# Finer waits ahead of seven TensorE products, and VectorE for the last imaginary part

## The reference

```
h = layer_norm(x)
for l in 0, 1:
    h = layer_norm(A*h + hybrid_mixer(h))            # three attention branches a, b, c, each projected, gated, summed
    h = layer_norm(A*h + memory_cross_attention(h))  # keys and values from 'mem' (256 x 1024)
    h = layer_norm(A*h + ffn)                        # l = 0: swiglu; l = 1: mixture of 8 experts
x = x + rmsnorm(even_mixer(rmsnorm(x)))              # dilated attention of 16 heads beside a state-space scan
x = x + rmsnorm(odd_mixer(rmsnorm(x)))               # pooling over windows, a gate, one last product
```

## Time and profile before

| | us |
|---|---|
| median of 3 runs | 2126.41 (2125.18 to 2128.82) |
| the profiled execution | 2124.61 |
| its span, first to last instruction | 2122.8 |

### The profile page before, as it was taken

One profiled execution on the slowest core, in us unless ns is written; L12 is line 12 of the kernel. 1 busy time (PEld: TensorE's weight loads), 2 busy tenths in 40 slices (PEclk: granted clock), 3 DMA queues, 4 the chain that ended last, 5 costly groups with the idle time before them and its releaser, 6 DMA issues.

```text
span 2122.8 us, 30291 instructions
## 1 busy us (share of the span) xinstructions
PE 2096.0 (99%) x13540; PEld 1251.1 (59%) x13540; DVE 785.6 (37%) x1430; ACT 323.9 (15%) x700; POOL 65.5 (3%) x72
## 2 busy tenths in 40 slices
PE   8999999999999999999999999999999999999998
PEld 4888786997468869753333333333333544855997
DVE  4325645556642276550100002001000489344446
ACT  2332121110123301210000000000000232420200
POOL 0000000000000000000000000000000035000000
PEclk9999999999999999999999999999999999999999
DMA  7524544444344245059999996999999832326340
GB/s 303 224 76 159 199 159 159 159 159 153 144 168 165 85 166 205 1 227 370 383 399 382 405 395 280 371 381 396 383 403 399 335 122 99 120 76 241 109 169 20
DMA packets 38453, 485.60 MB, mean 229 GB/s; under 512 B 4480, under 2 KB 4640, under 8 KB 7088
## 3 DMA queue, kind: packets, MB, share of 16 engines
q1 hardware_dynamic: 34848, 464.66, 54.8%
q0 software_dynamic: 3472, 18.95, 2.3%
HBM read 482.54 MB, written 1.05 MB: 228 GB/s over the span
## 4 chain that ended last, share of the span: by engine, by line
PE 92%; DVE 5%; ACT 1%; issue 1%; DMA 0%; POOL 0%; SPq 0%; DVEq 0%; ACTq 0%
PE bank L379 50%; PE pair L379 42%; DVE att L2411 2%; DVE att L2500 1%; DVE prob L2513 0%; DMA weights<-in_moe_down 0%; DVE prob L2411 0%; DVE att L2491 0%; DVE probT L2411 0%; DVE probT L2513 0%; ACT hT L2718 0%; DVE big L2461 0%; ACT big L2702 0%; DVE att L1584 0%; DMA const<-in_const 0%
## 5 line engine op out<-in xcount | busy, mean ns | idle before, releaser
L379 PE MATMUL bank<-weights,att 128*32 128x512 f32 (+1 forms) x4228 | 460.7, 593 | 0.3 <-DVE att L1584 0.2
L379 PEld LDWEIGHTS bank<-weights,att 128*32 128x32 f32 (+1 forms) x4228 | 137.6, 110 | 307.0 <-issue 307.0
L379 PE MATMUL bank<-hT,weights 128*128 128x256 f32 (+1 forms) x1232 | 246.9, 358 | 0.0
L379 PEld LDWEIGHTS bank<-hT,weights 128*128 128x128 f32 x1232 | 212.1, 190 | 31.5 <-issue 8.0
L379 PE MATMUL pair<-weights,big 128*32 128x512 f32 (+2 forms) x1606 | 224.5, 582 | 0.0
L2018 DVE TENSOR_TENSOR big<-head_gain,bank 128x256 f32<-128x256 f32 x66 | 27.8, 421 | 424.4 <-ACT head_gain L2913 424.4
L379 PEld LDWEIGHTS pair<-weights,big 128*32 128x32 f32 (+1 forms) x1606 | 82.9, 120 | 130.7 <-issue 128.4
L379 PE MATMUL pair<-weights,hT 128*128 128x512 f32 (+2 forms) x336 | 137.9, 568 | 2.5 <-ACT hT L2870 1.3
L2913 ACT ACTIVATE head_gain<-bank 128x256 f32<-128x256 f32 x66 | 25.4, 384 | 595.5 <-PE bank L379 595.5
L379 PEld LDWEIGHTS pair<-weights,hT 128*128 128x128 f32 x336 | 63.3, 190 | 72.5 <-issue 71.0
L379 PE MATMUL pair<-hT,weights 128*128 128x128 f32 (+1 forms) x784 | 105.0, 293 | 0.8 <-ACT hT L2718 0.8
(11 more groups left out here) (444 smaller groups left out, 2287.2 us busy)
## 6 DMA issues: line engine op xcount, KB each, us to landing
weights<-in_moe_up SPq DMA_DIRECT2D x88, 2048.0 KB, 11.2
weights<-in_moe_down SPq DMA_DIRECT2D x40, 2048.0 KB, 10.9
weights<-in_w_in SPq DMA_DIRECT2D x17, 2048.0 KB, 7.7
weights<-in_ffn_up SPq DMA_DIRECT2D x11, 2048.0 KB, 7.4
weights<-in_even_in SPq DMA_DIRECT2D x10, 2048.0 KB, 8.4
weights<-in_mem_wkv SPq DMA_DIRECT2D x8, 2048.0 KB, 7.7
weights<-in_odd_in SPq DMA_DIRECT2D x8, 2048.0 KB, 7.2
norm_par<-in_norms POOLq DMA_DIRECT2D x11, 1024.0 KB, 8.2
```

The costliest lines, as they stand in the source:

```text
L379: ins = pe.matmul(o, lhsT, rhs, **flags)
```

## The change

Nothing that is computed is left out. Seven edits refine waits or move work, and one moves work between engines:

1. Start: the transposes of row tile 0 go into four banks of two blocks; ScalarE signals every two blocks; `entry` waits every two k.
2. `projected` waits at first for value product `ready - 1`, and for `ready` only in front of k = nk-1 of its first block.
3. The key product of `cross` waits for each bank of `memT` when it comes to its k.
4. `seven_rows(("xo", l))` waits for head r's copy in front of the first product's r (as the mixer's `seven_rows` does with `merged`).
5. `few_sum` waits for each `few_down` copy in front of its first use.
6. Even heads: rounds 2 and 4 take 3 steps of filler; so two steps are left for round 8.
7. Scan: VectorE makes the imaginary part of block 7 behind the real part; GpSimd's loop ends at block 6. Where `outputs(7)` stands is as before.
8. End: the mean square of row tile 1 is split. Its three earlier quarters' part is worked out while part 4 is still multiplied; part 4's sum goes to a buffer of its own, ScalarE squares and sums it there, and takes the root with the earlier part as bias, while VectorE multiplies by the gain. The row is then finished and stored in two halves of 512 columns (256 KB each).

```diff
-            def rows_T(name, t, src):
+            def rows_T(name, t, src, blocks=4):
...
-                for j in range(2):
+                for j in range(KD // blocks):
                     o = begin(banks, (name, t, j))
-                    for i in range(4):
-                        ins = mm_t(o[:, i * P:(i + 1) * P], src(t, 4 * j + i), ident)
+                    for i in range(blocks):
+                        ins = mm_t(o[:, i * P:(i + 1) * P], src(t, blocks * j + i), ident)
...
-                        if c == 0 and k % 4 == 0:
-                            pe.wait_ge(*emptied((tname, t, k // 4)))
+                        blocks = 2 if in_halves and t == 0 else 4
+                        if c == 0 and k % blocks == 0:
+                            pe.wait_ge(*emptied((tname, t, k // blocks)))
...
-                pe.wait_ge(*emptied((("m", l), "value", ready)))
+                pe.wait_ge(*emptied((("m", l), "value", ready - 1)))
+
+                def column(k, i):
+                    if (k, i) == (nk - 1, 0):
+                        pe.wait_ge(*emptied((("m", l), "value", ready)))
...
-                pe.wait_ge(*emptied((("memT", l), KD - 2)))
...
+                def memT_ready(kk):
+                    if kk % 2 == 0:
+                        pe.wait_ge(*emptied((("memT", l), kk)))
+                product_T(("kT", l, 0), lambda kk: memT[:, kk, :], KD, ready=memT_ready)
...
-                pe.wait_ge(*emptied((("x", l), "value", 3)))
-                seven_rows(("xo", l), yT_at, xo_sums, xo_tokens, "xo_sums_ready")
+                seven_rows(("xo", l), yT_at, xo_sums, xo_tokens, "xo_sums_ready",
+                           lambda r: emptied((("x", l), "value", r)))
...
-                for q in range(2):
-                    pe.wait_ge(*emptied(("few_down", g, q)))
-                for i in range(2):
-                    pe.wait_ge(*emptied(("few_down", g, 2, i)))
...
+                            if t == 0:
+                                pe.wait_ge(*emptied(("few_down", g, q) if q < 2 else ("few_down", g, q, i)))
...
-                    fill(4)
+                    fill(3 if i in (2, 4) else 4)
...
+                    if b == SSM_TILES // 2 - 1:
+                        si = ssm_state[b % 2][:, 1, :, :]
+                        tt(tmpB, C, ri, ALU.mult)
+                        tt(tmpA, S, rr, ALU.mult)
+                        ve.tensor_tensor(si, tmpA, tmpB, ALU.add).then_inc(sems("im_ready"), 1)
...
+                    for a, z in ((0, D),) if t == 0 else ((0, D // 2), (D // 2, D)):
+                        ve.scalar_tensor_tensor(h[:, t, a:z], y_out[:, t, a:z], rstd[:, t, 0:1], h[:, t, a:z],
+                                                ALU.mult, ALU.add).then_inc(sems("rows_done"), 1)
...
+                        link(ve.tensor_copy(last_stats[:, 1, 2, :], last_stats[:, 1, 3, :]))
+                        link(ve.bn_aggr(mv[:, 1, :], last_stats[:, 1, 0:3, :]))
+                        link(ve.tensor_tensor(rstd[:, 1, 1:2], mv[:, 1, 0:1], mv[:, 1, 0:1], ALU.mult))
+                        link(ve.tensor_tensor(rstd[:, 1, 1:2], rstd[:, 1, 1:2], mv[:, 1, 1:2], ALU.add))
+                        link(ve.tensor_scalar(rstd[:, 1, 1:2], rstd[:, 1, 1:2], 0.75, RMS_EPS, ALU.mult, ALU.add))
                         weighted(1, c, 1)
                         ve.wait_ge(*filled(("do", c, 4)))
-                        link(ve.tensor_tensor(y_part(1, c, 0), u3, last[:, 256:512], ALU.add))
-                        measured(1, c, 0)
-                        row_variance(1)
-                        weighted(1, c, 0)
+                        ve.tensor_tensor(last_part, u3, last[:, 256:512], ALU.add).then_inc(sems("last_part_ready"), 1)
+                        ve.wait_ge(*L.next("last_part_ready"))
+                        link(ve.tensor_tensor(y_part(1, c, 0), last_part, g[:, 512 * c:512 * c + 256], ALU.mult))
                         row_out(1)
...
+                act.activation(spare[:, 6, :], spare[:, 5, :], ACT.Square, accum_out=rstd[:, 1, 2:3])\
+                   .then_inc(sems("scalar_step"), 1)
+                act.wait_ge(*L.next("scalar_step"))
+                act.activation(rstd[:, 1, 0:1], rstd[:, 1, 2:3], ACT.Sqrt, scale=1.0 / D, bias=rstd[:, 1, 1:2])\
+                   .then_inc(sems("root_ready"), 1)
...
-                for b in range(SSM_TILES // 2):
+                for b in range(SSM_TILES // 2 - 1):
...
+            parts = ((0, 0, D), (1, 0, D // 2), (1, D // 2, D))
+            for t, a, z in parts:
                 sp.wait_ge(*L.next("rows_done"))
-                sp.dma_start(rows[:, t, :], h[:, t, :]).then_inc(sems("out_stored"), 16)
-            sp.wait_ge(sems("out_stored"), 16 * NT)
+                sp.dma_start(rows[:, t, a:z], h[:, t, a:z]).then_inc(sems("out_stored"), 16)
+            sp.wait_ge(sems("out_stored"), 16 * len(parts))
```

More of the change, by code:

```diff
@@ L482, in entry @@
                         pe.wait_ge(*L.next(ready))
-                        rows_T(tname, t, src)
+                        rows_T(tname, t, src, 2 if in_halves and t == 0 else 4)
                     split = in_halves and (t, c) == (0, 0)
@@ L541, in product_T @@
                     for k in range(nk):
+                        if i == 0:
+                            ready(k)
                         at = k * 512 + i * P
@@ L676, in projected @@
                 s = next_tile()
-                pe.wait_ge(*emptied((("m", l), "value", ready)))
-                for half, i, k in halves(("p", l, branch), nk, lambda k, i: weights[:, s, k * D + i * P:k * D + i * P + P],
-                                         lambda k: yT[:, first + k, :]):
+                pe.wait_ge(*emptied((("m", l), "value", ready - 1)))
+                def column(k, i):
+                    if (k, i) == (nk - 1, 0):
+                        pe.wait_ge(*emptied((("m", l), "value", ready)))
+                    return weights[:, s, k * D + i * P:k * D + i * P + P]
+                for half, i, k in halves(("p", l, branch), nk, column, lambda k: yT[:, first + k, :]):
                     if (half, i, k) == (3, 1, nk - 1):
@@ L827, in mixer @@
                 banks.order, banks.next = [0, 1, 2, 3], 0
-                seven_rows(("o", l), lambda k, t: hT_at(k, t), wo_sums, wo_tokens, "wo_sums_ready", "merged",
-                           "wo_last_sum")
+                seven_rows(("o", l), lambda k, t: hT_at(k, t), wo_sums, wo_tokens, "wo_sums_ready",
+                           lambda r: L.next("merged"), "wo_last_sum")
             def cross(l):
@@ L959, in other_accumulators, with seven_rows @@
                 return outs
-            def seven_rows(name, rows, sums, tokens_of, ready, each_row=None, last_sum=None):
+            def seven_rows(name, rows, sums, tokens_of, ready, each_row, last_sum=None):
                 early, later = begin(pairs, (name, "A"), late=True), begin(pairs, (name, "B"), late=True)
@@ L979, in seven_rows @@
                     for r in range(4):
-                        if i == 1 and each_row:
-                            pe.wait_ge(*L.next(each_row))
+                        if i == 1:
+                            pe.wait_ge(*each_row(r))
                         a11, a12, a21, a22 = [rows(2 * r + x, t) for t in range(NT) for x in range(2)]
@@ L2590, in odd @@
                 for c in range(2):
-                    k1, k5, x, y, u3 = [spare[:, i, :] for i in range(5)]
+                    k1, k5, x, y, u3, last_part = [spare[:, i, :] for i in range(6)]
                     o, free = bank(("do", c))
@@ L2864, in _ @@
                     act.wait_ge(*L.next("columns_landed", 16))
-                for j in range(2):
+                blocks = 4 if t else 2
+                for j in range(KD // blocks):
                     act.wait_ge(*filled((("hT", "mix", 0), t, j)))
                     o, free = bank((("hT", "mix", 0), t, j))
-                    for i in range(4):
-                        k = 4 * j + i
+                    for i in range(blocks):
+                        k = blocks * j + i
                         ins = act.activation(hT[:, k, t * P:(t + 1) * P], o[:, i * P:(i + 1) * P], ACT.Identity,
@@ L3035, in _ @@
                         act.activation(spare[:, i, :], part, ACT.Copy).then_inc(sems("do_kept"), 1)
-                for t in range(NT):
-                    row_root(t)
+                row_root(0)
+                act.wait_ge(*L.next("last_part_ready"))
+                act.activation(spare[:, 6, :], spare[:, 5, :], ACT.Square, accum_out=rstd[:, 1, 2:3])\
[3 more added lines that the diff above has]
+                   .then_inc(sems("root_ready"), 1)
         @block.gpsimd
```

6 lines of the change are left out of this document (1 added, 5 removed).

## The result

| | before | changed | difference |
|---|---|---|---|
| median of 4 runs each, same chip | 2125.80 (2124.96 to 2128.82) | 2112.79 (2112.31 to 2115.36) | -13.0 |
| profiled execution | 2124.61 | 2112.48 | -12.1 |
| its span | 2122.8 | 2110.7 | -12.1 |

The ratio is 0.9939, with a 95% interval of 0.9922 to 0.9956: faster, by more than the 0.2% that the measurement tells apart. The forecast was 2115.4 with a low end of 2112.9, so the time fell 0.1 us outside the range, on the fast side.

The account below looks back on a forecast made before the run. TensorE was taken to bound the kernel, busy 2096.0 of 2122.8 us, leaving 26.8 us idle to win. Eight terms summed to 11.0 us, so 2126.41 - 11.0 = 2115.4 us, range 2112.9 to 2120.9.

Parts of the forecast that it names:

- Start: Kernel start: ScalarE copies sooner and TensorE waits for two copies, not four; gain 1.1 us, bounds 0.7 to 1.3.
- Projections: Projections, twice: three k in front cover the wait for VectorE's copy; gain 1.3 us, bounds 0.9 and 1.5.
- Keys: Key product, twice: waiting bank by bank for ScalarE's copies removes the idle time; gain 1.9 us, bounds 1.2 and 2.0.
- cross output: Cross output, twice: products of heads 0 to 2 cover the wait for head 3; gain 1.9 us, bounds 1.2 and 2.0.
- Expert sum: Expert sum, g = 1: three products now precede the last copy's first use; gain 1.2 us, bounds 0.6 and 1.3.
- scan: Scan end: VectorE makes six products alone at 0.72 us each, so TensorE starts sooner; gain 0.8 us.
- heads: Even heads, round 8: two filler steps cover the wait, rounds 2 and 4 not waiting; gain 1.7 us, bounds 0.8 and 1.8.
- End: Behind the last product: shorter finish 0.6 us, store in halves 0.5; together 1.1 us, bounds 0.5 and 1.8.
- Rival (c): Slower: TensorE spends more time at 1.2 GHz, as near 926; eight such spells give 2131.4 us; chance 0.02.
- Rival (a): Experts' stage: the weights' stream sets the pace, so earlier gains are waited off; 4.8 us left, 2121.6; chance 0.07.
- Rival (b): Some waits come back, or VectorE's scan products stay at 1.64 us; gain 6 to 8.5 us, 2118 to 2120.5; chance 0.15.
- rival (d): The waits named were not the ones that held; half the gain is missing: 5.5 us, 2120.9; chance 0.06.

Follow-up runs that it names:

- scan_shared: Changed kernel with GpSimd repeating the last scan block's three products into scratch, VectorE waiting for it; VectorE's products took 1.64 us, not 0.69, and TensorE's wait was 3.89 us.
- all_again2: The changed kernel, unchanged, run once more to count executions with and without a clock spell; median 2115.52 us.
- waits_only: The kernel before with edits 2 to 5 alone (projections, keys, cross output, expert sum); one execution, 2117.19 us.
- all_fill2: Changed kernel with two steps of the gates' filler moved from ahead of the even heads to in front of outputs(7); median 2111.46 us.
- wide_fill: Changed kernel with the router stage's unread 128-column products replaced by half as many of 512 columns; median 2117.07 us.
- router_dense: Changed kernel with further unread 512-column products put among the router's 8-column products; median 2117.35 us.

## Why the prediction was nearly right, and where it failed

Step by step:

- **Start.** Right: 1.10 of 1.1 us in the pair whose transposes took the same time, and 0.56 in the profiled one, where they took 0.6 us longer. ScalarE began 0.40 us sooner (8.90 to 8.50), as worked out.
- **Projections.** Right, 1.3 for 1.3: the loss was whole, and nothing was late next.
- **Keys, cross output.** Right in the mechanism, each sized 0.3 too low. The terms took the idle time plus 0.1; the earlier trace rows has 0.84 and 0.83, and 1.08 and 1.10 were won each time. Some 0.15 of it is the overlap of records, and 0.10 is the longer row behind a wait, which the prediction had no term for.
- **Expert sum, scan, heads.** 1.1 to 1.2, 0.8 and 1.6 to 1.7 for 1.2, 0.8 and 1.7. Round 3 keeps its 0.22 us, and rounds 2 and 4 wait for nothing. In the scan the choice of 0.72 for each product over 1.68 was right, and scan_shared shows why. The rule of the Trainium skill, GPSIMD Engine Reference, Specifications table, that GpSimd shares its SBUF interfaces with VectorE's instructions of two SBUF inputs, agrees with it.
- **End.** 1.2 for 1.1: root 0.8 (forecast 0.6 with the second part's 0.1 in it), halves 0.4 net. From the last sum to the end of the span it is 5.5 us, where the prediction had 5.2, and 6.7 before, where it had 6.3: it left out some 0.4 us on both sides, which cancels.
- **The sum.** 10.8 and 11.5 for 11.0. The fastest executions of the two kernels, 2122.71 and 2111.81, differ by 10.9. Edits 1 and 6 (start and even heads) had no run of their own; the leads alone carry them.

**The step that failed is the last one, from the sum to the time.** The prediction gave two figures: 2113.6 from the profiled execution, and 2115.4 from the median of three runs, and took the second. That median was itself a draw. Over 54 single executions before has a median of 2125.14 and a mean of 2125.89, with a spread of 2122.71 to 2130.42; 2126.41 was 1.3 us too high an anchor; from 2125.14 the same sum gives 2114.1, and the same range begins at 2111.6, below the 2112.79 measured. The changed kernel's 14 have 2112.98 and 2113.83. The means differ by 12.1 us (95% by resampling: 11.0 to 13.1), and the named edits account for 10.8 to 11.5 of it. The rest, 0.5 to 1.3, is within the interval: it needs no further cause, and none is shown. The 13.0 us between the medians of four could not have come from the edits: the upper bounds of the eight terms add up to 12.5 us, with 0.8 for the scan, and the range's gain of 13.5 had no term for the remainder.

**Rival (c) was built on one side only.** It read 0.57 in the earlier trace rows as something that the change might get more of. The same row says that before's own execution held a spell of 3 to 4 us, which the changed kernel's might lack; the range should have had some 1.3 us for it on the fast side, and a low end near 2111.6. The price of half a us for each us was about right: 3.5 us at the half clock cost 1.3 us, and some 10 us cost 4.0 to 4.4. Its sign of being wrong, more than 4 us at the lower clock, stands in all_again2 with some 10 us, in the changed kernel without a further edit; the sign tested the draw and not the change.

Rival (a) is out by waits_only; its premise was off too, for the experts' 128 tiles of 2 MB are 268 of the 485.6 MB that before's page counts, and not nearly all. Rival (b) is out by the rows of 0.69 us and rival (d) by the leads, which stand where each edit is. Whether the changed kernel draws spells more rarely than before stays open: 6 of its 14 executions lie within 0.9 us of its fastest, and 8 of 54 of before's, a difference that chance gives in some 3 of 100 cases. Mean clocks of 1.000 came 6 times in 14 and 2 times in the 50 of before whose clock is on record, but that figure also holds the fall behind the last product, and so doesn't count spells alone.

## What to carry to other kernels

Work out the gain of small edits from the leads between equal products of two traces, and not from medians, as soon as single executions lie further apart (here 7.7 us) than the gain. Put the sum against a pooled anchor, and give a clock spell in the trace of before room on both sides of the range. A wait for several copies in front of a product with several k is worth its whole idle time plus 0.1 to 0.3 us, if the work of the first k lasts longer than that wait.

## What the runs showed of the hardware

- Whether TensorE drops to 1.2 GHz after the same instructions, and for how long, differs from execution to execution: between 912 and 942 not at all, for some 3.5 us (cost 1.3), for some 7 us (0.83 granted from 912 to 932 in all_fill2, cost 2.9), or for some 10 us (cost 4.0 to 4.4). The medians of a kernel move by it more than by any of the eight edits. With 512-column work among the 8-column products none of five executions shows it in its time; with such work right behind them the profiled execution has it.
- Behind one wait of 3.89 us after a stretch of 512-column products 0.57 of the full clock was granted from 1800 to 1804 (scan_shared); behind waits of 1.08 and 1.89 us in the same place it was 1.00.
- At the start of the experts TensorE's weight loads stop for 0.90 to 1.67 us after the sixth, in every profiled execution but two, and the products then idle for up to 0.76 us; the profile names no releaser. The two are wide_fill and router_dense, which reach the place with another number of TensorE instructions behind them. The cause stays open.
- A float32 product of two SBUF inputs, 128 x 512, takes VectorE 0.69 us with GpSimd idle and 1.64 us with GpSimd at the same kind of work.
